# Three edits to a two-block transformer kernel: weight pieces of the modulation spread one to a step, attention scores computed by halves in turn, and one feed-forward for 768 tokens in place of two

## The reference

```python
# both blocks, D_FF = FFN_HIDDEN = 2816
x = x + ((silu(gate) * up) @ w_down[l])                        # block 1, 512 tokens
sh1, sc1, gt1, sh2, sc2, gt2 = split(s_lat @ ada_w[i] + ada_b[i], 6)   # s = silu(c); same for context
# block 2, layer 0: one set of weights for latent and context
x   = layernorm(ALPHA * x   + gt2  * swiglu(x   * (1 + sc2)  + sh2,  w_gate, w_up, w_down))
ctx = layernorm(ALPHA * ctx + gt2c * swiglu(ctx * (1 + sc2c) + sh2c, w_gate, w_up, w_down))
# block 2, layer 1: 8 heads, two score halves of 64 each, 768 keys, 512 queries
s = einsum('cbhqd,cbhkd->cbhqk', q * 64 ** -0.5, k)            # c = 0, 1
p = softmax(s); a = p[0] - lam_val * p[1]
o = einsum('bhqk,bhkv->bhqv', a, v)
```

## Time and profile before

| | us |
|---|---|
| Median of 3 runs (4545.06 to 4559.08) | 4546.12 |
| Profiled execution, its own time | 4552.97 |
| Span of its trace, first to last instruction | 4551.2 |
| PE busy (with its mean granted clock 0.912 of full speed) | 3889.8 |
| DVE busy | 2214.7 |
| ACT busy | 873.0 |
| POOL busy | 459.2 |

### The profile page before, as it was taken

How to read it: one execution, slowest core, us unless ns; L and a number is a source line. 1 busy time by engine, 2 the same in 40 slices (tenths; PEclk the granted TensorE clock), 3 DMA queues, 4 the chain that set the end, 5 groups by cost and what they waited for, 6 DMA issues and landing times.

```text
span 4551.2 us, 51386 instructions
## 1 busy us (share of the span) xinstructions
PE 3889.8 (85%) x21060; PEld 3234.8 (71%) x21060; DVE 2214.7 (49%) x3048; ACT 873.0 (19%) x1548; POOL 459.2 (10%) x408
## 2 busy tenths in 40 slices
PE   4988789979887899798979898769989599966997
PEld 3776566757765667588968897658879477655885
DVE  3435323544353235465546555553466743665346
ACT  1113100111131001223422342010110201421012
POOL 0001000000010000104520542110000100000000
PEclk8878899988698999799989999989999899988998
DMA  3210244222102443210001002112234321001222
GB/s 117 84 47 10 109 166 157 102 80 81 44 11 108 166 157 111 83 42 10 1 25 38 10 1 109 60 49 102 93 111 176 111 83 55 1 19 65 102 93 83
DMA packets 53307, 349.74 MB, mean 77 GB/s; under 512 B 6316, under 2 KB 7084, under 8 KB 14296
## 3 DMA queue, kind: packets, MB, share of 16 engines
q1 hardware_dynamic: 42336, 308.30, 18.6%
q10 hardware_dynamic: 10744, 38.18, 2.3%
HBM read 336.90 MB, written 9.56 MB: 76 GB/s over the span
## 4 chain that ended last, share of the span: by engine, by line
PE 72%; DVE 11%; DMA 7%; POOL 3%; ACT 3%; issue 1%; POOLq 1%; DVEq 0%; ACTq 0%; another core or an unknown queue 0%; SPq 0%
PE psum L496 18%; PE psum L497 17%; PE psum L498 17%; PE psum L1874 8%; DMA pieces_in<-pieces 6%; POOL xt_operands L648 2%; DVE pieces_lo L519 2%; PE psum L1872 1%; DVE pieces_hi L512 1%; PE psum L1061 1%; PE psum L1034 1%; PE psum L851 1%; PE psum L1045 1%; PE psum L1344 1%; DVE x_mem L2063 1%
## 5 line engine op out<-in xcount | busy, mean ns | idle before, releaser
L496 PE MATMUL psum<-xt_operands,pieces_hi 128*128 128x512 f32 (+1 forms) x2544 | 955.6, 376 | 182.1 <-DVE pieces_lo L519 180.1
L497 PE MATMUL psum<-xt_operands,pieces_hi 128*128 128x512 f32 (+1 forms) x2544 | 940.6, 370 | 0.0
L498 PE MATMUL psum<-xt_operands,pieces_lo 128*128 128x512 f32 (+1 forms) x2544 | 939.3, 369 | 0.0
L496 PEld LDWEIGHTS psum<-xt_operands,pieces_hi 128*128 128x128 f32 x2544 | 490.3, 193 | 301.2 <-DVE pieces_lo L519 205.1
L512 DVE CAST pieces_hi<-pieces_in 128x2048 fp32r<-128x2048 f32 x240 | 293.4, 1223 | 651.7 <-DMA pieces_in<-pieces 634.5
L519 DVE TENSOR_TENSOR pieces_lo<-pieces_in,pieces_hi 128x2048 fp32r<-128x2048 f32 x240 | 549.8, 2291 | 6.5
L497 PEld LDWEIGHTS psum<-xt_operands,pieces_hi 128*128 128x128 f32 x2544 | 490.6, 193 | 79.7 <-issue 2.6
L498 PEld LDWEIGHTS psum<-xt_operands,pieces_lo 128*128 128x128 f32 x2544 | 489.5, 192 | 80.2
L648 POOL TENSOR_TENSOR xt_operands<-xt_values,xt_operands 128x512 fp32r<-128x512 f32 (+1 forms) x128 | 153.7, 1230 | 2412.8 <-DVE xt_operands L639 2412.8
L496 PE MATMUL psum<-pieces_hi,xt_operands 128*128 128x512 f32 (+1 forms) x736 | 299.8, 407 | 73.4 <-DVE pieces_lo L519 73.4
L496 PE MATMUL psum<-pieces_hi,hidden_operands 128*128 128x512 f32 x792 | 312.9, 395 | 31.8 <-DVE hidden_operands L1304 27.3
(11 more groups left out here) (289 smaller groups left out, 5178.7 us busy)
## 6 DMA issues: line engine op xcount, KB each, us to landing
pieces_in<-pieces SPq DMA_DIRECT2D x294, 1024.0 KB, 4.8
arena<-mods ACTq DMA_DIRECT2D x8, 512.0 KB, 14.1
arena<-ln ACTq DMA_DIRECT2D x4, 1024.0 KB
x_park<-x_mem ACTq DMA_DIRECT2D x1, 3072.0 KB, 11.8
o_park<-arena ACTq DMA_DIRECT2D x2, 1536.0 KB
arena<-o_park ACTq DMA_DIRECT2D x1, 3072.0 KB
x_mem<-x_park ACTq DMA_DIRECT2D x1, 3072.0 KB, 18.9
arena<-line ACTq DMA_DIRECT2D x6, 448.0 KB, 6.0
```

The source lines that it names most:

```text
L496: signal_later(k, pe.matmul(out, sh, mh, start=start, stop=False))
L497: signal_later(k, pe.matmul(out, sh, ml, start=False, stop=False))
L498: return pe.matmul(out, sl, mh, start=False, stop=stop)
```

## The change

**Edit 1, the modulation pieces.** Two of the 24 pieces are used ahead of the first gate step, and one in each of the 22 steps. The stream of pieces is reordered to match. The silu of the conditioning vectors and the memset of their padding move one stage earlier (`cond_act`, `cond_pool`). The first two groups are taken by DVE at steps 7 and 15 and transposed one step later, the third is taken at step 21 and transposed inside the down phase (`late`).

**Edit 2, differential attention.** The query projection is stored with the factor -1/8 (`scale` of an activation that was there already), so that the row minimum of the scores is the bias of the exponential, and the scaling on DVE goes. PE computes both halves behind one wait, 512 keys of c = 0 and 1, then 256 of both. The scores rotate over three pairs of PSUM banks in place of two. The transposed blocks have one bank and go in two halves of three blocks, with the weighing of the unit before between them. The combination p0 + factor * p1 is cut in two: DVE does columns 0 to 383, POOL the columns 384 to 767 in two operations. The factor takes two small operations in place of three. The combination runs one unit behind the scores, the transposes two, the weighing three.

**Edit 3, one feed-forward for 768 tokens.** The two stages become one, `ffn_all_*`. 34 pieces (34 MB) are loaded and split once less; 294 pieces become 260. A gate step holds 2 x 8 x 3 products of 512 tokens and as many of 256. The down phase goes over six token tiles for each hidden tile; the rounded tiles have eight buffers, laid over the operands of the gate steps. ACT and DVE work on 768 columns at once.

```diff
+ADA_FIRST = ADA_PIECES - FT
-N_PIECES = 2 * (39 * DEPTH + 69)
+N_PIECES = 2 * (39 * DEPTH + 52)
 ...
-def ada_after(f):
-    return [n for n in range(ADA_PIECES) if n * 5 // 6 == f]
-ADA_TAKEN_AT = [ada_f + 1 for ada_f in (5, 12, 19)]
+ADA_BANK = (4, 5, 7)
+ADA_TAKEN_AT = (7, 15)
+ADA_TURNED_AT = (8, 16)
 ...
+    def between(f):
+        if f in ADA_TURNED_AT:
+            ada_turn_pe(k, pe, ADA_TURNED_AT.index(f), 6)
+        piece(ADA_FIRST + f)
+    for n in range(ADA_FIRST):
+        last = piece(n)
+    last.then_inc(S.ada_begun, 1)
+    ffn_pe(k, e, slot, k.both(NT1), k.hs, NT1, between, late)
 ...
+ALL_SEGS = ((0, 512), (512, 256))
+def ffn_all_pe(k, e, slot, _):
 ...
+        for half in range(2):
+            for s, (at, m) in enumerate(ALL_SEGS):
+                for kt in range(KT):
+                    last = product3(k, pe, k.ps[:, 4 * (f % 2) + 2 * half + s, 0:m], pair(w, slice(c, c + P)),
+                                    pair(xT, kt, slice(at, at + m)), kt == 0, kt == KT - 1)
 ...
+def ffn_all_dve(k, e, _):
 ...
+            if n < FT + 12:
+                if f % 4 == 1:
+                    piece = split_dve(k, e, n, with_lo=False)
+                if f % 4 == 2 or f == FT - 1:
+                    split_lo_dve(k, e, n, piece)
+            if c == 1 and f == 3:
+                gated_add_dve(k, e, range(0, NT2), 2, 0, NT2, lambda n: n % 8)
 ...
+    def scores(u):          # da_pe
+        if u >= 2:
+            pe.wait_ge(S.p_ready, 2 * u - 1)
+        for at, m, _ in SEGS:
+            for c in range(2):
+                last = pe.matmul(da_scores(k, u, c)[:, at:at + m], k.aq[rows, h, i * P:(i + 1) * P],
+                                 k.ak[rows, h, at:at + m], start=True, stop=True)
+    def turn(v, part):
+        if part == 0:
+            pe.wait_ge(S.combined, v + 1)
+            pe.wait_ge(S.combined_pool, v + 1)
+        if v or part:
+            pe.wait_ge(S.pt_ready, 2 * v + part)
+        for j in range(3):
+            last = pe.transpose(k.ps[:, 6, j * P:(j + 1) * P], k.ap[v % 3][:, 0, at:at + P], k.ident)
 ...
+            scores(u)
+            turn(u - 2, 0)
+            weigh(u - 3)
+            turn(u - 2, 1)
 ...
+def da_pool(k, e, _):
+    for u in range(len(AUNITS)):
+        pool.wait_ge(S.factor_ready, u + 1)
+        p = k.ap[u % 3][:, :, HALF_KEYS:KEYS]
+        e.link(pool.tensor_tensor(p[:, 1, :], p[:, 1, :], k.afac[:, u:u + 1].broadcast_to([P, HALF_KEYS]), ALU.mult))
+        pool.tensor_tensor(p[:, 0, :], p[:, 0, :], p[:, 1, :], ALU.add).then_inc(S.combined_pool, 1)
```

More of the change, by code:

```diff
@@ L387, in _ @@
                                  .rearrange("a p n -> (a p) n")).then_inc(S.full[i], 16)
+            for i in range(N_PIECES % RING):
+                sp.wait_ge(S.empty[i], 1)
+                sp.sem_clear(S.empty[i])
+                sp.dma_start(k.ring[i], src[N_PIECES - N_PIECES % RING + i]).then_inc(S.full[i], 16)
         @block.tensor
@@ L1249, in ffn_pe @@
             w = take_split(k, pe, slot, FT + 6 * c + part)
+            if late and c == 1 and part == 3:
+                late()
             for i in range(min(4, FT - 4 * part)):
@@ L1283, in ffn_act, with ffn_dve @@
                        ACT.Copy).then_inc(S.hs_hi_ready, 1)
-def ffn_dve(k, e, silu, hid, hs, nt, finish, skipped=lambda f: 0, between=None):
+def ffn_dve(k, e, silu, hid, hs, nt, finish, skipped=lambda f: 0, between=None, late=None):
     dve, S = e.eng, k.S
@@ L1313, in ffn_dve, with ada_turn_pe @@
                 finish(range(0, nt))
+            if late and c == 1 and f == 16:
+                late()
     finish(range(nt, 2 * nt))
-def ada_after(f):
-    return [n for n in range(ADA_PIECES) if n * 5 // 6 == f]
-ADA_TAKEN_AT = [ada_f + 1 for ada_f in (5, 12, 19)]
-ADA_TURNED_AT = [ada_f + 1 for ada_f in ADA_TAKEN_AT]
+ADA_BANK = (4, 5, 7)
+ADA_TAKEN_AT = (7, 15)
+ADA_TURNED_AT = (8, 16)
+def ada_turn_pe(k, pe, group, bank):
+    S = k.S
+    pe.wait_ge(S.ada_taken, group + 1)
+    if group:
+        pe.wait_ge(S.ada_tr_taken, group)
+    for blk in range(4):
+        last = pe.transpose(k.ps[:, bank, P * blk:P * blk + P], k.ada_out[:, group, P * blk:P * blk + P], k.ident)
+    last.then_inc(S.ada_tr, 1)
@@ L1352, in ffn1_pe, with piece @@
-    ffn_pe(k, e, slot, k.both(NT1), k.hs, NT1, ada)
-def ffn1_act(k, e, _):
+    def piece(n):
+        group, kt = divmod(n, KT)
+        w = take_raw(k, pe, slot)
+        for j in range(4):
+            last = pe.matmul(k.ps[32 * j:32 * j + 32, ADA_BANK[group], :], k.cond32[:, kt, :],
+                             w[:, 512 * j:512 * j + 512], start=kt == 0, stop=kt == KT - 1)
+            signal_later(k, last)
+        piece_used(k, slot, split=False)
+        if kt == KT - 1:
+            last.then_inc(S.ada_ps, 1)
+        return last
@@ new lines, in scores, with weigh @@
+                if at:
+                    last.then_inc(S.s_ps, 1)
+    def turn(v, part):
[5 more added lines that the diff above has]
+        for j in range(3):
+            at = HALF_KEYS * part + j * P
+            last = pe.transpose(k.ps[:, 6, j * P:(j + 1) * P], k.ap[v % 3][:, 0, at:at + P], k.ident)
+        last.then_inc(S.pt_ps, 1)
+    def weigh(v):
+        h, i = AUNITS[v]
+        pe.wait_ge(S.pt_ready, 2 * v + 2)
+        if v:
+            pe.wait_ge(S.ov_taken, v)
+        for j in range(NT2):
+            last = pe.matmul(k.ps[:, 7, 0:P], k.apt[v % 2][:, j * P:(j + 1) * P], k.av[:, j, h * P:(h + 1) * P],
+                             start=j == 0, stop=j == NT2 - 1)
+        last.then_inc(S.ov_ps, 1)
@@ new lines, in da_act @@
+    for u in range(n + 2):
+        for c in range(2):
+            if u >= 2 and c == 0:
+                turned_half(u - 2, 0)
+            if u < n:
+                act.wait_ge(S.o_ps, 2 * u + c + 1)
+                if u >= 3 and c == 0:
+                    act.wait_ge(S.pt_ps, 2 * (u - 2))
+                act.activation(k.ap[u % 3][:, c, :], da_scores(k, u, c), ACT.Exp, bias=k.amin[:, 2 * u + c:2 * u + c + 1],
+                               scale=-1.0, accum_out=k.asum[:, 2 * u + c:2 * u + c + 1]).then_inc(S.p_ready, 1)
+            if u >= 2 and c == 1:
+                turned_half(u - 2, 1)
@@ L2515, in da_dve @@
 def da_dve(k, e, _):
     dve, S = e.eng, k.S
[L2517 to L2535 removed]
+    n = len(AUNITS)
```

302 lines of the change are left out of this document (174 added, 128 removed).

## The result

The changed kernel takes 4377.36 us (median of 4 runs, 4372.94 to 4378.32), the kernel before in all its runs beside it 4546.51. The ratio is 0.9617, with a 95% interval of 0.9605 to 0.9629: clearly faster. The forecast was 4370 in a range of 4352 to 4403.

What follows compares the result with a forecast made beforehand. The prediction took PE as the bound, holding 72% of the chain of waits and losing time where it waits. Gains of 89 + 34 + 53 = 176 us take 4552.97 to 4377, less 6.85 gives 4370, range 4352 to 4403.

Steps and rivals of the forecast that it cites:

- the last step: Whole kernel: 6.85 us taken off the forecast profiled time of 4377 to predict the median, 4370.
- Late loads: Gate steps of block 1: three late loads allowed in 21 steps, 0.6 us each, adding 1.6 us.
- The rival of late single steps: Gate steps: every single step loses 0.6 us to a late load, 22 us in all, 4392; chance 9%.
- stall: Down phase of the feed-forward, turn of the chunk: PE loses 4.5 us waiting for the fourth hidden tile.
- The price of POOL's two operations: Attention: two POOL operations of 384 columns take 1.0 us each, 2.1 together, bounds 0.9 and 3.3.
- The 0.4 for the collision: Attention: 0.4 us added to POOL's two operations for collisions with DVE, making 2.5.
- the second loop: Attention, over two units: scores to factor, POOL's operations, transposes, weighing, transposes; 7.7 us, 3.85 for one unit.
- the sum for PE's own work: Attention: PE's scores 1.5, transposes 0.71 and weighing 1.5 make 3.7 us for a unit.
- the first loop: Attention: scores, minimum of c = 0, exponential, next scores; 3.4 us for a unit.
- The first rival: Attention: the score halves don't run side by side, scores take 2.6 us, gain 24 not 53, 4399; chance 7%.
- POOL and DVE hold each other off: Attention: DVE's half combination waits 1.1 us for POOL, unit 4.5, gain 33, 4390; chance 17%.
- POOL's broadcast operand: Attention: POOL reading the factor as a broadcast could make its operations slow, kernel slower than before, 4623 at 6 us each; 2%.

Runs made afterwards that it cites:

- edit 1 alone: The kernel before with only the modulation pieces reordered, one to a step and two in front; 4466.16 us, ratio 0.9811.
- turn_first: The changed kernel, with DVE doing low parts of four hidden tiles and gated additions before the next piece's cast at the down-phase turn; 4371.91 us.
- dve_combines: The changed kernel with the whole combination of 768 columns on DVE and nothing on POOL; 4374.53 us, ratio 0.9606.
- dve_early: dve_combines, with the first score product of half 0 no longer waiting for the previous unit's exponential of half 0; 4378.82 us, ratio 0.9617.
- edit 2 alone: The kernel before with only the differential attention change; 4496.81 us, ratio 0.9875.
- pool_256: The changed kernel with POOL combining 256 of the 768 columns in place of 384, DVE 512; 4376.09 us, ratio 0.9606.

## Why the prediction was right

**The sum.** 176 us forecast, 176.5 between the two profiled executions. That these agree so closely is luck. The three terms measure 85.7, 29.0 and 59.0 in the traces, 173.7 together: two were too large, by 3.3 and 5.0, and one too small, by 6.0. The 2.8 left over lie in stretches that the sum didn't price, within their spread from run to run. The mechanisms of edits 1 and 3 were right in the main. The 7 us by which the median is above 4370 come from the last step: I took off 6.85, by which the profiled execution of before lay above its median. In every later comparison the kernel before had its median at 4552 to 4553.5. The profiled one was no outlier, and 4377 was the better number.

**Edit 1**, 89 forecast, 85.7 in the trace (42.5 and 43.2), 85.9 alone. The step of 12.11, the transposes (0.43) and the absence of a cost at the front held. Late loads cost 3.2 and 2.7 us in a layer where I allowed 1.6; with 1.3 and 2.5 with edit 1 alone my allowance was at the low end of the spread. I had taken late loads for chance; they come at the same five steps in every run. The rival of late single steps (22 us) is far off. What I had put at most at 1 us, that PE is warm in step 0, is up to 2.4: in layer 2 the first gate products now take 1370.75 to 1381.95, 11.2 us, before 1414.77 to 1428.40, 13.6.

**Edit 3**, 34 forecast, 29.0 in the trace, 30.9 alone. Gate steps (16.68), tiles, gap (2.8) and stall (3.96 for 4.5) are close to what was worked out. The mis-sized term is what comes behind a wait: the sum took the waits themselves and not the products at half clock. Some nine of them at 0.43 in place of 0.23 make 1.8 us at the gap, and 2.8 went with the stall when turn_first took it away. With the stall as measured the sum is 554.1 + 1.8 + 2.8 = 558.7; steps of 16.68 in place of 16.64 add 0.8, and 559.5 was measured.

**Edit 2**, 53 forecast, 59.0 in the trace (unit 3.70 in place of 3.85), 55.2 alone. The price of POOL's two operations was right in the sum (0.83 + 1.27 = 2.1) and wrong in what came on top. The 0.4 for the collision is already inside the 1.27: DVE's combination ends at 3787.57, POOL's addition began at 3787.15, so it stood still for 0.42 and has 0.85 of its own, if it stood still for all of the overlap. With 2.18 in place of 2.5 the second loop gives 3.70, the same as the sum for PE's own work (3.7, measured 3.64), which the prediction had as its bound below. The statement that the second loop, through POOL, sets the unit is not borne out: with POOL out of it (dve_combines), or the wait of the first loop loosened (dve_early), the unit stays at 3.70. In the changed kernel POOL's addition and ACT's second copy of the unit before both end just ahead of the first transposes (3784.65 and 3784.67, the transposes' loads start at 3784.78), so without POOL the copy still holds them. What ends last is PE's own work, 3.64, and in every second unit ACT's copy behind it, by the loop of 3.70 that the prediction didn't have. I had also put DVE's work at 3.4 in a unit, and it is 2.9 (28.62 in ten); nothing hung on it. Of the 6.0 by which this term was too small, 4.7 are the 0.15 in 31 units, the rest filling and draining. That edit 2 alone brings less, 55.2, lies for the most part with the clock at the start of its stage.

**The rivals.** The first rival, scores of 2.6 us, is out: they take 1.5, and in either order. That POOL and DVE hold each other off is real, as the rule of the Trainium skill ("SBUF — State Buffer", "Who interferes with whom") says and the 0.42 shows. But it is POOL that waited: DVE's combination starts 0.2 us ahead of POOL's addition, and POOL's multiplication had run beside a minimum that reads PSUM. DVE is held off only where POOL starts within 0.04 us of it (in pool_256 its 512 columns take 1.27, where 384 take 0.61 and 768 take 1.01 alone). Even then the unit didn't change, so the 4390 of that rival had no ground: DVE has 0.8 us to spare in a unit. POOL's broadcast operand was no danger: 0.83 for 384 columns.

## What to carry to other kernels

When a loop through several engines is shortened, work out PE's own sum first: here it was 3.64 of a unit of 3.70, other loops lay at 3.5 to 3.7, and four changes to them brought nothing. A variant that changes nothing shows only that the loops that it touches don't end last alone, and a variant that does change something points at every loop in which its instruction lies. What paid was one more pair of banks, so that the scores needn't wait for the second exponential of the unit just before, and one load for each step, so that a ring of three hardly ever runs dry. And price a longer wait of PE as the wait plus the products at half clock behind it, here two thirds as much again (2.8 and 1.8; 3.96 in two pieces and 2.8). The first piece of the latter, 1.96 us, had no half clock behind it.

## What the runs showed of the hardware

A DVE operation with two SBUF inputs and a POOL operation hold each other off, and the wait shows as a longer instruction, not as idle time. In 31 units POOL's addition took 1.26 to 1.27 us where DVE's combination of 0.61 had started 0.2 before it. In the last unit, when POOL's multiplication starts at nearly the same time, it is DVE's that takes twice as long, although its row starts 0.04 us ahead of POOL's (timelines of POOL and DVE in the changed kernel):

```profile
3844.11 0.83 POOL L2721 TENSOR_TENSOR xt_values<-xt_values 128x384 f32<-128x384 f32 x1 [0.18 <-DVE xt_values L2706]
3845.01 1.20 POOL L2722 TENSOR_TENSOR xt_values<-xt_values 128x384 f32<-128x384 f32 x1
```

```profile
3844.07 1.28 DVE L2713 SCALAR_TENSOR_TENSOR xt_values<-xt_values 128x384 f32<-128x384 f32 x1
```

The one that is held off doesn't wait for the whole length of the other, as the prediction quoted the rule: in pool_256 DVE's 512 columns end 0.55 us after POOL's addition, in the last unit here its 384 end 0.41 after POOL's multiplication, and 384 take 0.61 alone. Nor does the order of the starts in the rows decide it in the last unit. Spans on POOL are rough, so these differences are estimates.

DVE's minimum over PSUM (0.95) leaves POOL alone, which then keeps its 0.83.

Modulation products in front take the half clock upon themselves. Behind a wait of 8.69 us they run slowly (16 in 3.64, granted clock 0.50, where eight take 1.07 in the running stage), but the gate products behind them are at full clock after the first (1.00 from 1371.64 on). In the kernel before, the first twelve gate products, 5.3 us, went by at a granted clock of 0.50 (timeline of PE, layer 2, one line of three; changed, then before):

```profile
1367.02 3.64 PE L1368 MATMUL psum<-pieces_in,xt_values 128*32 128x512 f32 x16 [8.69 <-DMA pieces_in<-pieces]
1370.75 0.59 PE L505 MATMUL psum<-xt_operands,pieces_hi 128*128 128x512 f32 x1
...
1371.64 0.40 PE L505 MATMUL psum<-xt_operands,pieces_hi 128*128 128x512 f32 x1
```

```profile
1414.77 0.80 PE L496 MATMUL psum<-xt_operands,pieces_hi 128*128 128x512 f32 x1 [12.90 <-DVE pieces_lo L519]
...
1420.06 0.44 PE L496 MATMUL psum<-xt_operands,pieces_hi 128*128 128x512 f32 x1
```
